# Convolution taps on VectorE around the weight split for the keys, and the position of the convolution's tanh

## The reference, cut to what matters

```python
def conformer_conv(z, w, bias, ln_g, ln_b):
    a, g = jnp.split(z, 2, axis=-1)
    u = a * jax.nn.sigmoid(g)
    y = lax.conv_general_dilated(u, w[:, None, :], window_strides=(1,), padding=[(15, 15)],   # 31 taps, 512 channels
                                 dimension_numbers=("NWC", "WIO", "NWC"), feature_group_count=CONV_WIDTH_2) + bias
    return jax.nn.silu(layer_norm(y, ln_g, ln_b))

def mixer_stream(parts, lp, cos, sin, ctx_kv, lam, lam_init):
    zf, zconv, zgq, zgk, zgv, zdq, zdk, zdv, zgate = parts          # parts of hx @ w_in
    y_four = fourier_mix(zf) @ lp["w_four"]
    y_conv = conformer_conv(zconv, ...) @ lp["w_conv"]
    ...                                                             # grouped attention, differential attention
    gates = jax.nn.sigmoid(zgate.reshape(b, l, N_BRANCH, D_MODEL))
    ys = jnp.stack([y_four, y_conv, y_gqa, y_diff], axis=2)
    return jnp.sum(gates * ys, axis=2) @ lp["w_out"]
```

## Time and profile before

| | |
|---|---|
| median of 3 runs | 2316.47 us (2301.54 to 2328.40) |
| the profiled execution, its time | 2310.77 us |
| the profiled execution, its span | 2308.9 us |
| mean granted TensorE clock | 0.926 |
| PE busy | 2048.5 us (89%) |
| VectorE busy | 1070.1 us (46%) |
| ScalarE busy | 762.6 us (33%) |
| GpSimd busy | 1071.8 us (46%) |
| HBM read | 266.10 MB, 117 GB/s |

### The profile page before, as it was taken

The page is one execution under the profiler, slowest core; times in us unless marked ns, Lnnn a source line. Parts: engine busy times, 40 slices in busy tenths (PEclk is TensorE's granted clock), DMA queues, the critical chain, the costliest instruction groups (busy, mean ns, idle before and its releaser), DMA issues. The chain is left out here.

```text
span 2308.9 us, 32999 instructions
## 1 busy us (share of the span) xinstructions
PE 2048.5 (89%) x13789; PEld 1785.6 (77%) x13789; DVE 1070.1 (46%) x1772; ACT 762.6 (33%) x1208; POOL 1071.8 (46%) x519
## 2 busy tenths in 40 slices
PE   2968899997999989979987999999787878888997
PEld 2546899986878778967775888888686867888997
DVE  7742444037465647484235111114468575634114
ACT  2324344332222442252222222222333423443442
POOL 7001768856364214403342444444464342576885
PEclk6778999997999999999998999999797988999999
DMA  5771667665412103102331223323323231254552
GB/s 136 251 178 60 222 215 251 209 221 187 135 37 82 56 28 110 55 28 73 125 104 55 91 79 104 110 64 119 107 85 110 65 101 55 85 191 136 167 186 87
DMA packets 292647, 274.78 MB, mean 119 GB/s; under 512 B 13770, under 2 KB 290772, under 8 KB 292196
## 3 DMA queue, kind: packets, MB, share of 16 engines
q1 hardware_dynamic: 289076, 266.71, 37.3%
q10 hardware_dynamic: 2688, 4.86, 0.7%
q0 software_dynamic: 736, 1.12, 0.4%
HBM read 266.10 MB, written 4.19 MB: 117 GB/s over the span
## 5 line engine op out<-in xcount | busy, mean ns | idle before, releaser
L2107 POOL TENSOR_TENSOR wl<-raw,wh 128x1024 fp32r<-128x1024 f32 (+3 forms) x452 | 1019.4, 2267 | 1095.8 <-ACT wh L713 1094.4
L713 ACT CAST wh<-raw 128x1024 fp32r<-128x1024 f32 (+3 forms) x452 | 420.8, 937 | 836.8 <-PE gb L2135 459.0
L2133 PE MATMUL gb<-xh,wh 128*128 128x256 f32 (+1 forms) x1920 | 639.0, 333 | 41.8 <-DVE xl L976 16.7
L2134 PE MATMUL gb<-xl,wh 128*128 128x256 f32 (+1 forms) x1920 | 630.5, 328 | 0.0
L2135 PE MATMUL gb<-xh,wl 128*128 128x256 f32 (+1 forms) x1920 | 629.9, 328 | 0.0
L2133 PEld LDWEIGHTS gb<-xh,wh 128*128 128x128 f32 x1920 | 372.3, 194 | 84.7 <-issue 25.0
L2135 PEld LDWEIGHTS gb<-xh,wl 128*128 128x128 f32 x1920 | 373.3, 194 | 29.6
L2134 PEld LDWEIGHTS gb<-xl,wh 128*128 128x128 f32 x1920 | 373.8, 195 | 28.2
L1188 PE MATMUL gb<-wh,xh 128*128 128x256 f32 x608 | 176.5, 290 | 7.9 <-POOL wl L2107 7.9
L1657 DVE SCALAR_TENSOR_TENSOR cy<-upad,vecs,cy 128x512 f32<-128x512 f32 (+1 forms) x240 | 178.7, 817 | 0.1
L1189 PE MATMUL gb<-wh,xl 128*128 128x256 f32 x608 | 174.3, 287 | 0.0
(11 more groups left out here) (409 smaller groups left out, 3145.9 us busy)
## 6 DMA issues: line engine op xcount, KB each, us to landing
raw<-in_w_in SPq DMA_DIRECT2D x62, 1024.0 KB, 5.5
raw<-in_w_ada SPq DMA_DIRECT2D x48, 1024.0 KB, 5.6
raw<-in_w_ffn SPq DMA_DIRECT2D x44, 1024.0 KB, 5.3
raw<-in_mlp_w SPq DMA_DIRECT2D x32, 1024.0 KB, 5.5
raw<-in_w_ffn SPq DMA_DIRECT2D x16, 768.0 KB, 4.8
raw<-in_w_ffn SPq DMA_DIRECT2D x16, 640.0 KB, 4.4
raw<-in_ssm_w_glu SPq DMA_DIRECT2D x8, 1024.0 KB, 5.6
raw<-in_w_out SPq DMA_DIRECT2D x8, 1024.0 KB, 5.1
```

The lines of the kernel that those rows point to most:

```text
L713: nc.scalar.copy(split_half(wh, p, j, h), raw_half(p, it, j, h)).then_inc(hi_ready, 1)
L2107: nc.gpsimd.tensor_tensor(split_half(wl, p, j, h), raw_half(p, it, j, h), split_half(wh, p, j, h).bitcast(F32), ALU.subtract)\
L2133: nc.tensor.matmul(g[:, b, :], H[:, k, :], XH, start=st, stop=False)
L2134: nc.tensor.matmul(g[:, b, :], H[:, k, :], XL, start=False, stop=False)
```

## The change

Four things are changed. (1) The 44 early taps are cut: VectorE issues 12, then waits on `w_ready` and issues the rest. In layer 0 it waits until GpSimd has split the block of the keys, in layer 1 until it has also split the next block, the first of the queries. (2) In layer 1 the rest is 48, not 32, so that 60 taps are early; the gaps of branch 0 hold 2 instead of 5 and those of branch 2 hold 9 instead of 12, and 27 instead of 25 are left to the end. Layer 0's portions stay. (3) On ACT `conv_tanh` is called ahead of the second block of `dv`, ahead of its rounding and its copy. (4) `heads_act` hands the callback through. All taps are on VectorE in both kernels.

```diff
-        def heads_act(act, l, name, nt, more=None):
+        def heads_act(act, l, name, nt, more=None, ahead_of=None):
...
-            gemm_act(act, p, evac)
+            gemm_act(act, p, evac, ahead_of)
...
             heads_act(act, l, "dk", 4, conv_squares)
-            heads_act(act, l, "dv", 4)
-            conv_tanh()
+            heads_act(act, l, "dv", 4, ahead_of=lambda it, j: conv_tanh() if j == 1 else None)
             transposes_act(act, l, "d")
...
-            TAPS_EARLY, TAPS_DFT, TAPS_0, TAPS_2, HEAD_STEPS = (44, 20, 4, 11, 4) if ns == 2 else (44, 4, 5, 12, 2)
+            TAPS_FIRST, TAPS_EARLY, TAPS_DFT, TAPS_0, TAPS_2, HEAD_STEPS = \
+                (12, 32, 20, 4, 11, 4) if ns == 2 else (12, 48, 4, 2, 9, 2)
...
+            taps(TAPS_FIRST)
+            dve.wait_ge(w_ready, 2 * (q["gkv"].m0 + (1 if ns == 2 else 2)))
             taps(TAPS_EARLY)
             all_drained(dve, q["gkv"])
```

## The result

| | before | after |
|---|---|---|
| median | 2313.27 us (2295.21 to 2341.14, 20 runs) | 2290.74 us (2278.26 to 2306.59, 20 runs) |
| span of the profiled execution | 2308.9 us | 2303.6 us |
| mean granted TensorE clock there | 0.926 | 0.934 |

The ratio is 0.9911, with an interval of 0.9887 to 0.9934: 20.6 us less (15 to 26; the plain medians are 22.5 apart). Timed again later, beside the last experiments, the changed kernel had 2296.52 us (2273.31 to 2306.96) against 2313.67, ratio 0.9904 (0.9869 to 0.9939). Forecast were 2294 us and a gain of 19.0.

What follows compares the result with a forecast made beforehand. PE, busy 89%, was bounded by its waits and slow clock, with VectorE the bound in layer 1's branches 0 and 2. 5.1 + 2.7 + 2.6 + 2.8 + 3.3 + 2.5 = 19.0 us off 2313.6 gave 2294, range 2274 to 2310.

Steps and rivals of the forecast that it cites:

- Layer 0, early taps: Layer 0, keys: PE's wait for the keys' split passes, 3.5 us, and its slow clock, 1.6 us; 5.1 us in all.
- no idle time, no slow clock: Layer 0, keys' products: without PE's wait they run at full clock, 11.5 us instead of 13.1, gaining 1.6 us.
- Layer 1, early taps and branch 0: Layer 1: queries' second-block split ends sooner, 2.7 us (0 to 5.9); shorter gaps of branch 0, 2.6 us (0 to 6.9).
- Layer 1, branch 2: 61 taps become 54 before `s_cy`, with as many splits between; 2.8 us (0 to 7.8).
- The sum of both engines: Layer 1, branch 2: VectorE and GpSimd exclude each other, so the stage lasts their summed work; 7 fewer taps save 2.8 us.
- rival A: Layer 1, last 27 taps: the four `dk` splits stand until the run ends, saving 8.4 us more; 2286 us, chance 0.20.
- The tanh: Ahead of differential attention: moved tanh lets head splits start sooner; 3.3 us in layer 0, 2.5 in layer 1, clock included.
- B: Branches 0 and 2: PE and ACT set the pace, so shorter gaps pay nothing; 13.6 us gain, 2299 us, chance 0.15.
- C: Layer 0: the queries' first block is split late, so the 5.1 us go to PE's next wait; 2299 us, chance 0.08.
- D: Layer 1: the 48 taps are held at 1.11 us each, delaying the keys' norm; 14.3 us loss, 2328 us, chance 0.05.
- turning point of 0.81: Layer 1, 48 early taps: at 0.81 us a tap, ending at 1727.9, the change would turn from gain to loss.
- E: Splits slip in between taps anyway, so early taps pay neither 5.1 nor 2.7 us; 11.2 us left, 2302 us, chance 0.03.

## Why the prediction was right

**Layer 0, early taps (5.1).** 5.11, and 5.11 with this part alone; 0.35 of it is gone by the grouped attention. The keys' products begin 3.93 us sooner behind the first tap (3.5 forecast) and take 11.91 us (672.68 to 684.59 on PE) instead of 13.09, so the clock gave 1.2 of the 1.6 I had put down to it. (The four splits of the earlier trace rows end 9.2 us behind the taps, not 9.6; nothing hangs on it.) What the tenth hides is scatter. The mechanism repeats: PE's wait is 3.35 to 3.52 us in the four profiles without this edit and gone in the seven with it. The size doesn't: the four have 45.07 to 47.74 us from first tap to keys, as the keys' products last 11.58 to 14.24 us with the slow clock behind the wait, and the seven have 41.48 (four) or 39.78 (three), as the DFT lasts 8.80 or 7.11 us. That I compared with a 46.59 and a 41.48 was luck. My "no idle time, no slow clock" holds for the keys (1.00 in 672 to 684) but not for the DFT ahead of them.

**Layer 1, early taps and branch 0 (2.7 + 2.6).** Together 6.29 against 5.3. The step in which I credited branch 0 with its shorter gaps holds only with its other side: its 2.4 us are what the 16 extra early taps cost ahead of the keys, and the wait with the old portions brings the same 99.34. So the whole of the 6.3 is the wait's. Of my two terms the first is short by 0.6. The splits of the queries' second block end 2.76 us sooner behind the first tap (37.05 against 39.81), as worked out. But the first operation of the norm slips in ahead of them, 3.88 us sooner, right behind the last tap (1716.32, 0.29 us); the next two are held beside them (2.17 us each). At the fourth L1608 3.28 us are left (37.43 against 40.71). The other 3.0 come in the branch (2.6 forecast).

**Layer 1, branch 2 (2.8).** 3.38 in the first profile, 11.9 in the second. The sum of both engines, which I reckoned with, is right for a held run: those with 54 taps behind the grouped attention and a held end took 102.77 and 102.93 us, those with 61 took 106.14 to 106.17. For a free one rival A's 8.4 come on top, here 8.5. Which of the two the first profile would show I couldn't know.

**The tanh (3.3 + 2.5).** PE's waits fell by 3.09 in layer 0 and about 2.2 in layer 1, as worked out (3.1 and 2.3). Only 2.07 of the first show in the stage, because the half-clock stretch in this branch was longer in that profile. These are the windows from 972 to 981 of the kernel after and, below them, the matching ones of before, 962 to 971 (last numbers: granted clock, DMA share, GB/s):

```profile
972.00:975.00 3.00, 3.00 (x15) 3.00 (x15) 1.25 (x2) 0.36 (x1) 3.00 (x2) 0.50 0.00 0
975.00:978.00 3.00, 3.00 (x16) 3.00 (x15) 2.51 (x12) 0.00 (x0) 0.25 (x1) 0.50 0.48 165
978.00:981.00 3.00, 3.00 (x24) 3.00 (x23) 2.90 (x8) 0.00 (x0) 0.00 (x0) 0.88 0.06 18
```

```profile
962.00:965.00 3.00, 3.00 (x20) 3.00 (x20) 2.30 (x2) 0.02 (x1) 2.94 (x2) 0.69 0.00 0
965.00:968.00 3.00, 3.00 (x22) 3.00 (x20) 2.54 (x12) 0.00 (x0) 0.00 (x0) 0.74 0.53 173
968.00:971.00 3.00, 3.00 (x28) 3.00 (x26) 2.90 (x8) 0.00 (x0) 0.00 (x0) 1.00 0.03 10
```

PE is busy through all of them and yet runs at half its clock for a time, with no idle time before. Over the windows shown the granted clock falls short of 1.00 by 3.4 us' worth after and by 1.7 before: 1.7 us lost, as much as this kernel is slower there than the one with the tanh alone (215.10 against 213.42). Without the change this stage took 216.5 to 223.8 us in six profiles, with it 212.7 to 219.3 in eight: a scatter as large as the gain.

**The total.** That the gain of 20.3 us in one pair of profiles lies so near to 19.0 is partly luck: among the profiles layer 0 up to its keys moves by 1.7 us with the wait (the clock in the DFT), grouped to differential in layer 0 by up to 7 and the last stage by up to 7, in variants of either kernel, and no run tells why for all of it. What carries the forecast is the ratio over 20 executions each, 15 to 26 us, and the waits, which repeat.

**The rivals.** A came true in some executions, and in the changed kernel itself: its place and cause were right, and so was its price in the stage (8.5 us), but at the end 3.4 us were left of it. B fails: branch 0 gives back 2.2 us for its shorter gaps, though the early taps had cost as much, and branch 2 is shorter by 3.4. C fails, as PE's wait for `wl` is gone in both layers with nothing in its place. D fails at its price: 48 taps took 19.10 us, 0.398 each, and even where a pair of splits got in, 23.28, or 0.49, far from the turning point of 0.81. E fails for the kernel before. By the rule of the Trainium skill that I weighed there ("SBUF — State Buffer", section "Who interferes with whom"), whoever issues first gets the shared pair of ports for its whole instruction, so that the other would wait for one instruction; the runs agree while VectorE's run is young (5.14 us for a pair against 4.78 undisturbed) and not when it is older (28.74 for four).

## What to carry to other kernels

Where VectorE runs many like instructions back to back, look when GpSimd asks within the run: with the taps and splits of this kernel, a request in the first seven or so costs VectorE one instruction's hold-up per split, a later one costs GpSimd the rest of the run. Cut the run where the other engine's work is due; a wait on that work does it, and so does a mere stop on VectorE's own last result, for 0.12 us. A stage that comes and goes between executions of one kernel (here by 8.5 us) can be such a race near its edge, so profile twice before a stage's gain is believed.

## What the runs showed that I had not expected

- The edge is sharp and lies near 7.3 taps. Counted from the last split's end or the last stop, the splits got in at ages of 2.03, 2.27, 2.75 and 2.91 us (5.1 to 7.3 taps of 0.398) and at 3.9 us (5.9 taps of 0.665), and were shut out at 2.90, 2.95, 3.36 and 3.45 us (7.3 to 8.7 taps) and at 6.18 (9.3 of 0.665). 2.90 and 2.91 fell on different sides. What counts to it in the chip no run here shows.
- Tiny operations are held as well: the second L1608, 128x128, took 2.17 us in the profile after and 2.18 before, beside a split, where the fourth took 0.28 in both. So the work between the keys and branch 0 is no safe place for splits either.
- TensorE's clock fell to 0.50, the lower of its two levels (1.2 of 2.4 GHz), in stretches in which PE had been busy without a break (972 to 978 above), and for different lengths in two executions of nearly the same work (about 3.4 and 6.8 us, worked out from the windows above).
